# Second block: transposing and normalising rows in one product with a diagonal matrix

## The chip, the cores and the metric

The program runs on 1 core of one Trainium2 chip. The metric is device time in microseconds (us) of one launch. Engines are named as in the profile: PE is TensorE's matmul, PEld its weight load, DVE VectorE, ACT ScalarE, POOL GpSimd, SP SyncE.

## The reference, cut to what matters

Two transformer blocks run one after the other on 256 tokens of width 1024, in float32. The first block (a convolution branch, a gated linear attention branch, a mixture of 64 experts) ends in a layer norm. The second block normalises its rows three times and multiplies each result by large matrices:

```
def _rmsnorm(x, g):
    x32 = x.astype(jnp.float32)
    y = x32 * lax.rsqrt(jnp.mean(x32 * x32, axis=-1, keepdims=True) + EPS)
    return (y * g.astype(jnp.float32)).astype(x.dtype)

xn = _rmsnorm(x, mix_norm[l]);  h = xn @ w_in[l]          # input projections
...
x = x + merged @ w_out[l]
xn = _rmsnorm(x, ffn_norm[l]);  up = xn @ w_up[l]         # feed-forward
x = x + (jax.nn.gelu(g_ffn) * up[..., D_FF:]) @ w_down[l]
g_ple = jax.nn.sigmoid(_rmsnorm(x, ple_norm[l]) @ w_ple_gate[l])
x = x + g_ple * (p[l] @ w_ple_proj[l])
```

Every row (token) has one factor, 1/sqrt(mean of squares + 1e-6); every column (channel) has one gain. PE contracts over the partition dimension, so the rows, which lie with tokens on partitions, have to be transposed to channels on partitions before each of these products.

## The kernel before

The 256 tokens are two tiles (t = 0, 1) of 128 partitions; `tok(10)` holds the rows x of both, 1024 floats each. The engines run five separate instruction streams in the order in which the code is written and meet by semaphores; there is no scheduler. PSUM is 8 banks of 128 x 512 floats, given to tasks in rotation (`take_bank`, `full`, `wait_full`, `read`).

The second block's normalisation happens in three stages: stage 0 before the input projections (tasks `x2t0` to `x2t3`), stage 1 before the feed-forward (`x3t0` to `x3t3`), stage 2 before the last gate (`x4t0` to `x4t3`). Tasks 0 and 1 are the two halves of 4 channel blocks of tile 0, tasks 2 and 3 those of tile 1. For every stage and tile:

- ACT squares both halves of the rows with a running sum (`rms_square`, L1359) and takes the root (`rms_root`, L1365); DVE scales the first half's sum (`rms_shifted`, L2015) and inverts the root (`rms_inverse`, L2020). The result is one factor per partition.
- The rows are multiplied by that factor, 128 x 512 at a time: on ACT (`rms_scale`, L1371), and for tile 1 of stage 0 on DVE (L2076). Each pass increments the semaphore `xn_half`.
- PE transposes 8 blocks of 128 x 128 (`turn_normed`, L731), 4 to a bank, against the identity; each half waits for its own `xn_half`.
- ACT copies each bank out with the column gain, rounded to the form that PE reads fast (`take_turned`, L1380), and DVE writes what the rounding left (`low_turned`, L2065). That releases the bank, and the next product of PE (`kiwi_k` in stage 0, `fg0_0` in stage 1, `pg0_0` in stage 2, lines L644 and L689) waits for tasks 0 and 2 before its first channel block and for 1 and 3 before its fifth (`as_turned`).

Around them: in stage 0 DVE first finishes the layer norm of the first block (`last_norm`: L2027, L2034, L2038, L2041, L2046), whose tile 1 is interleaved with the factor of tile 0. In stage 1 PE runs the four products `mo0_0`, `mo1_0`, `mo0_1`, `mo1_1` of the output projection, and tile 0 is turned between `mo0_1` and `mo1_1`. In stage 2 tile 0 is turned after `dn1_1`, then PE does 8 matmul instructions of `pp` (L1153), then tile 1, then `pp` again, then `pg`. A product called through `mm` on plain float32 operands appears in the trace as two MATMUL and two LDWEIGHTS instructions; a call of `nc.tensor.transpose` on float32 appears as one of each (the transposes of L731 are 48 calls in the code and 48 records; the products of L1096 are 16 calls and 32 records).

Of the kernel before, what the change touches and what calls it, by code (L numbers as in the profile page):

```python
# [7 lines left out]
ALU = mybir.AluOpType  # L8
# [7 lines left out]
P = 128  # L16
# [131 lines left out]
def build(nc, a, out):  # L148
    with ExitStack() as ctx:
        def sb(name, shape, dt=F32):  # L150
            return ctx.enter_context(nc.sbuf_tensor(name, shape, dt))
# [36 lines left out]
        e_idx = sb("e_idx", [P, TT, 8], U32)  # L188
        over = sb("over", [P, 1], I32)
        bias_dram = nc.dram_tensor("bias_scratch", (NH, 512), F32, kind="Internal").ap()  # L190

# [428 lines left out]
        def _(pe):  # L620
# [102 lines left out]

            def turn_normed(src, pre, stage, t):

                for k in range(2):
                    pe.wait_ge(S("xn_half"), 4 * stage + 2 * t + k + 1)
                    o = take_bank(f"{pre}t{2 * t + k}")
                    for i in range(4):
                        c = 4 * k + i  # L730
                        last = nc.tensor.transpose(o[:, P * i:P * i + P], src[:, t, P * c:P * c + P], ident[:])  # L731
                    full(last, f"{pre}t{2 * t + k}")
# [289 lines left out]
            for t in range(TT):  # L1022
                turn_normed(tok(1), "x2", 0, t)
            kiwi_parts = (kiwi_high.rearrange("p (c n) -> p c n", c=DC),
# [76 lines left out]
            for t in range(TT):  # L1101
# [10 lines left out]
                for k in range(2):  # L1112
                    o = take_bank(f"pv{t}_{k}")
                    for s in range(t + 1):
# [8 lines left out]
            tile_by_tile([unit(1), unit(1)], merged2_parts, "mo", arrive=as_counted("merged_low", 4),  # L1123
                         between={(1, 1): lambda: turn_normed(tok(4), "x3", 1, 0)})
            turn_normed(tok(4), "x3", 1, 1)
            for i in range(6):
# [21 lines left out]
            for t in range(TT):  # L1148
                turn_normed(tok(4), "x4", 2, t)
                for u in range(2):  # L1150
                    o = take_bank(f"pp{u}_{t}")
                    for c in range(2):
                        last = mm(o[:], pT[:, c, P * t:P * t + P], w[:, c, 512 * u:512 * u + 512],  # L1153
                                  start=c == 0, stop=c == 1)
                    full(last, f"pp{u}_{t}")
# [6 lines left out]
        def _(act):  # L1162
# [204 lines left out]

            def rms_scale(stage, t, h):
                cut = slice(512 * h, 512 * h + 512)
                act.wait_ge(S("rms_inverse"), 2 * stage + t + 1)  # L1370
                A(tok(4 if stage else 1)[:, t, cut], tok(10)[:, t, cut], ACT.Copy, scale=rms_factor(stage, t)  # L1371
                  ).then_inc(S("xn_half"), 1)

            def take_turned(pre, js, gain):
# [14 lines left out]
            rms_root(0, 0)  # L1389
            rms_scale(0, 0, 0)  # L1390
            ln_root(1)
            rms_scale(0, 0, 1)
            take_turned("x2", [0], "mix_norm")
# [149 lines left out]
            rms_root(1, 0)  # L1543
            rms_scale(1, 0, 0)
            rms_scale(1, 0, 1)
            wait_read(act, "mo0_1")
# [7 lines left out]
            rms_root(1, 1)  # L1554
            rms_scale(1, 1, 0)
            rms_scale(1, 1, 1)
            take_turned("x3", [2, 3], "ffn_norm")
# [31 lines left out]
            for t in range(TT):  # L1589
                wait_read(act, f"dn1_{t}")  # L1590
                rms_square(2, t, 1)
                rms_root(2, t)
                rms_scale(2, t, 0)
                rms_scale(2, t, 1)
                if t:
                    wait_landed(act, 1, "pg1_1")
                    wait_used(act, "dn1_1")
                    weights_high_half(1, "pg1_1", 0)
                take_turned("x4", [2 * t, 2 * t + 1], "ple_norm")
# [10 lines left out]
        def _(dve):  # L1610
# [406 lines left out]

            def rms_inverse(stage, t):
                dve.wait_ge(S("rms_root"), 2 * stage + t + 1)
                v.reciprocal(rms_factor(stage, t), rms_factor(stage, t)).then_inc(S("rms_inverse"), 1)  # L2020

            def last_norm(t):
# [8 lines left out]
                if t:  # L2031
                    rms_inverse(0, 0)
                dve.wait_ge(S("ln_bn"), 2 * k + 2)
# [36 lines left out]
            low_turned("x2", [0], "mix_norm", 0)  # L2070
            rms_inverse(0, 1)
            dve.wait_ge(S("rms_inverse"), 2)
            dve.wait_ge(S("x2_ready"), 4)
            for h in range(2):
                cut = slice(512 * h, 512 * h + 512)
                ts(tok(1)[:, 1, cut], tok(10)[:, 1, cut], rms_factor(0, 1), None, ALU.mult).then_inc(S("xn_half"), 1)  # L2076
            low_turned("x2", [1, 2, 3], "mix_norm", 0)
# [152 lines left out]
            residual("mo", 1, 0)  # L2230
            rms_inverse(1, 0)
            residual("mo", 0, 1)
            low_turned("x3", [0, 1], "ffn_norm", 1)
            rms_shifted(1, 1)
            residual("mo", 1, 1)
            rms_inverse(1, 1)
            low_turned("x3", [2, 3], "ffn_norm", 1)
# [59 lines left out]
            residual("dn", 1, 0)  # L2297
            rms_inverse(2, 0)
            residual("dn", 1, 1)
            low_turned("x4", [0, 1], "ple_norm", 2)  # L2300
            rms_inverse(2, 1)
            take_pp(0)
# [114 lines left out]
```

## Time and profile before

| | us |
|---|---|
| median of 3 runs | 1723.84 (1721.44 to 1726.67) |
| the profiled execution, its own time | 1723.52 |
| its span | 1721.8 |
| PE busy | 1363.8 (79% of the span) |
| DVE busy, ACT busy, POOL busy | 445.4, 446.4, 608.5 |
| mean granted clock of PE | 0.889 of full speed |
| second block, from the end of the experts to the end | about 1206 to 1721.8 |
| PE's share of the chain that ended last | 65% |

The page lists engines' busy times, groups of instructions with what ended the idle time before them, and the chain of work that ended last. A stage is read in the timeline, which gives start, duration and, in brackets, the idle time of the engine before the row and who ended it.

### The profile page before, as it was taken

What the parts mean: (1) busy time and instruction counts of PE and PEld (TensorE: products, weight loads), DVE (VectorE), ACT (ScalarE), POOL (GpSimd) and SP (SyncE); (2) the same over time, 40 slices, a digit from 0 to 9 for tenths busy, and PEclk for the clock granted to TensorE, in tenths of its full rate; (3) what the DMA queues carried; (4) which work ended last, traced back from release to release, by engine and by line L of the source; (5) the groups of instructions that cost most, each with busy time, mean ns of one, the idle gap of its engine ahead of it and who ended that gap; (6) DMA issues with size and microseconds to landing.
All of it is one profiled execution on the core that took longest, in us unless ns stands there. A gap on an engine that the chain in (4) does not pass through costs nothing.

```text
span 1721.8 us, 21025 instructions
## 1 busy us (share of the span) xinstructions
PE 1363.8 (79%) x8812; PEld 965.2 (56%) x8812; DVE 445.4 (26%) x973; ACT 446.4 (26%) x602; POOL 608.5 (35%) x484
## 2 busy tenths in 40 slices
PE   7999998966647755774667576657799999899998
PEld 7899996433313322331333133212699989788886
DVE  3995545100000000000000000000416643355303
ACT  4454741000000000000000000000548554655534
POOL 6886691000000000000000000000587968698894
PEclk9999998988778878886888788778799999999999
DMA  9443469999999999999999999999445444455551
GB/s 362 155 175 120 174 253 367 405 426 424 427 428 429 429 428 429 428 428 429 429 427 430 429 428 429 427 428 418 163 173 205 157 172 147 147 196 189 182 192 50
DMA packets 46505, 539.52 MB, mean 313 GB/s; under 512 B 4504, under 2 KB 8608, under 8 KB 15200
## 3 DMA queue, kind: packets, MB, share of 16 engines
q1 hardware_dynamic: 43296, 533.00, 75.9%
q0 software_dynamic: 1040, 3.38, 0.5%
q10 hardware_dynamic: 2096, 2.11, 0.4%
q8 instruction: 53, 0.87, 0.2%
q14 instruction: 20, 0.16, 0.0%
HBM read 537.41 MB, written 1.06 MB: 313 GB/s over the span
## 4 chain that ended last, share of the span: by engine, by line
PE 65%; DMA 28%; DVE 2%; ACT 2%; SPq 1%; issue 1%; POOL 1%; DVEq 0%; ACTq 0%
PE bank L644 30%; DMA ring<-in_w 16%; PE bank L897 13%; DMA slab<-in_w 10%; PE bank L877 6%; PE bank L689 5%; PE bank L694 3%; PE bank L957 3%; DMA ring<-in_units 1%; SPq L422 1%; PE bank L946 1%; POOL ring_parts L583 1%; PE bank L916 1%; ACT ring_parts L1187 0%; PE bank L1069 0%
## 5 line engine op out<-in xcount | busy, mean ns | idle before, releaser
L583 POOL TENSOR_TENSOR ring_parts<-ring,ring_parts 128x512 fp32r<-128x512 f32 x448 | 594.5, 1371 | 136.4 <-ACT ring_parts L1187 136.3
L897 PE MATMUL bank<-ring,slab 128*32 128x512 f32 x1472 | 252.5, 669 | 152.5 <-DMA ring<-in_w 79.2
L644 PE MATMUL bank<-slab_parts,ring_parts 128*128 128x256 f32 x2560 | 357.1, 284 | 0.4 <-DVE slab L2185 0.4
L644 PEld LDWEIGHTS bank<-slab_parts,ring_parts 128*128 128x128 f32 x2560 | 336.0, 192 | 2.4 <-DVE slab L2185 1.2
L596 POOL TENSOR_TENSOR slab_parts<-slab,slab_parts 128x1088 fp32r<-128x1088 f32 x1 | 2.5, 2476 | 818.7 <-ACT slab_parts L1319 818.7
L946 PE MATMUL bank<-ring,slab 128*32 128x512 f32 x736 | 139.6, 726 | 142.0 <-DMA ring<-in_w 80.3
L897 PEld LDWEIGHTS bank<-ring,slab 128*32 128x32 f32 x1472 | 68.9, 122 | 316.5 <-issue 315.1
L1187 ACT ACTIVATE ring_parts<-ring 128x2048 fp32r<-128x2048 f32 x114 | 211.9, 1910 | 94.6 <-PE bank L644 92.7
L946 PEld LDWEIGHTS bank<-ring,slab 128*32 128x32 f32 x736 | 37.1, 130 | 228.1 <-issue 227.4
L644 PE MATMUL bank<-ring_parts,slab_parts 128*128 128x512 f32 (+1 forms) x672 | 160.4, 388 | 3.9 <-POOL ring_parts L583 2.9
L1964 DVE TENSOR_TENSOR slab<-slab,bank 128x512 f32<-128x512 f32 x16 | 11.0, 688 | 551.8 <-PE bank L897 551.8
L644 PEld LDWEIGHTS bank<-ring_parts,slab_parts 128*128 128x128 f32 x672 | 125.7, 190 | 31.6 <-POOL ring_parts L583 3.7
L897 PE MATMUL bank<-slab 128*32 128x512 f32 x512 | 128.7, 661 | 1.4 <-DMA ring<-in_w 1.4
L877 PEld LDWEIGHTS bank<-slab 128*128 128x128 f32 x512 | 124.3, 334 | 8.2 <-issue 5.0
L877 PE MATMUL bank<-slab 128*128 128x128 f32 x512 | 123.2, 399 | 1.5 <-DVE slab L1947 1.5
L689 PE MATMUL bank<-slab_parts,ring_parts 128*128 128x512 f32 x384 | 97.9, 397 | 2.1 <-DVE slab_parts L2065 2.1
L644 PE MATMUL bank<-rows_parts,ring_parts 128*128 128x256 f32 x368 | 91.4, 285 | 0.0
L1642 DVE SCALAR_TENSOR_TENSOR bank<-slab,cols,bank 128x255 f32<-128x255 f32 (+28 forms) x232 | 88.0, 464 | 0.1
L1307 ACT ACTIVATE slab<-bank 128x512 f32<-128x512 f32 x16 | 9.6, 597 | 286.1 <-PE bank L897 271.8
L1315 ACT ACTIVATE slab<-bank 128x512 f32<-128x512 f32 x16 | 9.6, 597 | 283.7 <-PE bank L946 283.7
L1972 DVE COPY slab<-bank 128x512 f32<-128x512 f32 x16 | 11.1, 691 | 278.0 <-PE bank L946 278.0
L1303 ACT ACTIVATE slab<-bank 128x512 f32<-128x512 f32 x16 | 9.6, 597 | 271.5 <-PE bank L897 248.8
(312 smaller groups left out, 1322.7 us busy)
## 6 DMA issues: line engine op xcount, KB each, us to landing
ring<-in_w SPq DMA_DIRECT2D x142, 2048.0 KB, 19.8
ring<-in_units SPq DMA_DIRECT2D x59, 2048.0 KB, 8.3
slab<-in_w SPq DMA_DIRECT2D x48, 2048.0 KB, 25.1
ring<-in_units SPq DMA_DIRECT2D x2, 1024.0 KB, 9.1
slab<-in_w SPq DMA_DIRECT2D x2, 1024.0 KB, 21.3
slab<-bias_scratch ACTq DMA_DIRECT2D x2, 1024.0 KB, 8.5
slab<-in_xT SPq DMA_DIRECT2D x1, 1024.0 KB, 5.1
rows<-in_ln_g POOLq DMA_DIRECT2D x2, 512.0 KB, 16.6
```

What stands on the lines that cost most here:

```text
L422: sp.dma_start(slot(step, j), src.rearrange("e (p c) n -> p (e c n)", p=P)).then_inc(S(f"expert_landed{step % 2}{j}"), 16)
L583: ins = g.tensor_tensor(r32(w_q), w_q, r32(high_q), ALU.subtract)
L644: return mm(out_, l, r, start=start and first, stop=stop and last)
L689: mm(o[:].rearrange("p (a t) -> p a t", a=2), r32(high[:, c, cut]), r32(xn3_both[:, :, T * c:T * c + T]), start=c == 0, stop=c == DC - 1)
L694: last = mm(o[:, 0:T], r32(low[:, c, cut]), r32(xn3_parts[0][:, c, :]), start=False, stop=c == DC - 1, skip_group_check=True)
L877: last = mm(b[:, P * (c % 4):P * (c % 4) + P], tok(0)[:, t, c::DC], sel[:, t, :, :].rearrange("p j s -> p (j s)"), start=t == 0, stop=t == 1)
L897: last = mm(b[CAP * j:CAP * j + CAP, :], xg[:, c, CAP * j:CAP * j + CAP], wt[j][c], start=c == 0, stop=c == DC - 1, tile_position=(0, CAP ...
L916: last = mm(gate_bank[CAP * j:CAP * j + CAP, :], xg[:, c, CAP * j:CAP * j + CAP], wt[:, j, i, :], start=c == 0, stop=c == DC - 1, tile_pos ...
L946: last = mm(b[CAP * j:CAP * j + CAP, :], hid_t[:, m, CAP * j:CAP * j + CAP], wt[j][:, 512 * hf:512 * hf + 512], start=m == 0, stop=m == 3, ...
L957: last = mm(acc[t][hf][:], spread[:, P * t:P * t + P], y_sb[:, 512 * hf:512 * hf + 512], start=False, stop=ends, skip_group_check=again)
L1187: A(r32(high), w, ACT.Copy).then_inc(S("high_ready"), 1)
L1642: ins = stt(out_, src[:, c, 0:T - lag], wc, sum_[:, lag:T], ALU.mult, ALU.add)
```

## The change

The passes that scale the rows are gone. Instead DVE multiplies the 128 x 128 identity by the row factors into a new tile, `turner[:, t, :]`, right after it has inverted the root, and PE multiplies the unscaled rows by that diagonal matrix: the result of `rows.T @ diag(factor)` is the transposed and scaled block. The call is `mm`, an ordinary float32 product, in place of `nc.tensor.transpose`. PE waits for `turner_ready` once per tile and no longer once per half.

```
-            def turn_normed(src, pre, stage, t):
-
+            def turn_normed(pre, stage, t):
+
+                pe.wait_ge(S("turner_ready"), 2 * stage + t + 1)
                 for k in range(2):
-                    pe.wait_ge(S("xn_half"), 4 * stage + 2 * t + k + 1)
                     o = take_bank(f"{pre}t{2 * t + k}")
                     for i in range(4):
                         c = 4 * k + i
-                        last = nc.tensor.transpose(o[:, P * i:P * i + P], src[:, t, P * c:P * c + P], ident[:])
+                        last = mm(o[:, P * i:P * i + P], tok(10)[:, t, P * c:P * c + P], turner[:, t, :],
+                                  start=True, stop=True)
                     full(last, f"{pre}t{2 * t + k}")
...
-            def rms_scale(stage, t, h):
-                cut = slice(512 * h, 512 * h + 512)
-                act.wait_ge(S("rms_inverse"), 2 * stage + t + 1)
-                A(tok(4 if stage else 1)[:, t, cut], tok(10)[:, t, cut], ACT.Copy, scale=rms_factor(stage, t)
-                  ).then_inc(S("xn_half"), 1)
-
...
             rms_root(0, 0)
-            rms_scale(0, 0, 0)
             ln_root(1)
-            rms_scale(0, 0, 1)
             take_turned("x2", [0], "mix_norm")
...
             rms_root(1, 0)
-            rms_scale(1, 0, 0)
-            rms_scale(1, 0, 1)
...
             rms_root(1, 1)
-            rms_scale(1, 1, 0)
-            rms_scale(1, 1, 1)
...
                 rms_root(2, t)
-                rms_scale(2, t, 0)
-                rms_scale(2, t, 1)
...
-            def rms_inverse(stage, t):
+            def rms_turner(stage, t):
                 dve.wait_ge(S("rms_root"), 2 * stage + t + 1)
                 v.reciprocal(rms_factor(stage, t), rms_factor(stage, t)).then_inc(S("rms_inverse"), 1)
+                dve.wait_ge(S("rms_inverse"), 2 * stage + t + 1)
+                ts(turner[:, t, :], ident[:], rms_factor(stage, t), None, ALU.mult).then_inc(S("turner_ready"), 1)
...
                 if t:
-                    rms_inverse(0, 0)
+                    rms_turner(0, 0)
                 dve.wait_ge(S("ln_bn"), 2 * k + 2)
...
             low_turned("x2", [0], "mix_norm", 0)
-            rms_inverse(0, 1)
-            dve.wait_ge(S("rms_inverse"), 2)
-            dve.wait_ge(S("x2_ready"), 4)
-            for h in range(2):
-                cut = slice(512 * h, 512 * h + 512)
-                ts(tok(1)[:, 1, cut], tok(10)[:, 1, cut], rms_factor(0, 1), None, ALU.mult).then_inc(S("xn_half"), 1)
+            rms_turner(0, 1)
```

All six calls of `rms_inverse` become `rms_turner`, at the same places.

On DVE in stage 0 (the end of the first block's layer norm for tile 1, interleaved with tile 0's factor) there stands before, `bank` and `rows` being the layer norm's operands and `small` the factors:

```order
L2030 BN_STATS small<-bank 128x6
L2020 RECIPROCAL small<-small 128x1 [waits rms_root]
L2034 BN_AGGR small<-small 128x2 [waits ln_bn]
L2038 SCALAR_TENSOR_TENSOR bank<-bank,small,rows 128x512 [waits ln_stats]
L2015 TENSOR_SCALAR small<-small 128x1 [waits rms_sum]
L2065 SCALAR_TENSOR_TENSOR rows_parts<-bank,cols,slab_parts 128x128 [waits xn_high,bank_full6]
L2020 RECIPROCAL small<-small 128x1 [waits rms_root]
L2076 TENSOR_SCALAR slab<-slab,small 128x512 [waits x2_ready,rms_inverse]
L2076 TENSOR_SCALAR slab<-slab,small 128x512
```

The same places on DVE after the change:

```order
L2020 BN_STATS small<-bank 128x6
L2008 RECIPROCAL small<-small 128x1 [waits rms_root]
L2010 TENSOR_SCALAR turner<-ident,small 128x128 [waits rms_inverse]
L2024 BN_AGGR small<-small 128x2 [waits ln_bn]
L2028 SCALAR_TENSOR_TENSOR bank<-bank,small,rows 128x512 [waits ln_stats]
L2003 TENSOR_SCALAR small<-small 128x1 [waits rms_sum]
L2055 SCALAR_TENSOR_TENSOR rows_parts<-bank,cols,slab_parts 128x128 [waits xn_high,bank_full6]
L2008 RECIPROCAL small<-small 128x1 [waits rms_root]
L2010 TENSOR_SCALAR turner<-ident,small 128x128 [waits rms_inverse]
```

For tile 0 a 128 x 128 instruction has moved in ahead of the layer norm's aggregate for tile 1; for tile 1 it takes the place of two 128 x 512 passes.

On PE in stage 1, with the end of `mo0_1`, the turning of tile 0 and the start of `mo1_1`, there stands before:

```order
L644 MATMUL bank<-ring_parts,slab_parts 128x512 [waits low_ready]
L731 MATMUL bank<-ident,slab 128x128 [waits bank_read1,xn_half]
L731 MATMUL bank<-ident,slab 128x128 x3
L731 MATMUL bank<-ident,slab 128x128 [waits bank_read6,xn_half]
L731 MATMUL bank<-ident,slab 128x128 x3
L644 MATMUL bank<-ring_parts,slab_parts 128x512 [waits high_ready,bank_read7]
```

The same place on PE after the change (each row here is a call; the float32 product is two instructions on the chip):

```order
L645 MATMUL bank<-ring_parts,slab_parts 128x512 [waits low_ready]
L732 MATMUL bank<-turner,slab 128x128 [waits bank_read1,turner_ready]
L732 MATMUL bank<-turner,slab 128x128 x3
L732 MATMUL bank<-turner,slab 128x128 [waits bank_read6]
L732 MATMUL bank<-turner,slab 128x128 x3
L645 MATMUL bank<-ring_parts,slab_parts 128x512 [waits high_ready,bank_read7]
```

Nothing moved against its neighbours; the second half of the tile lost its wait for a pass, and the operand is the diagonal.

## Rows read from the trace of the kernel before

**Rows 1.** The page, engines' busy time: us, share of the span, instructions.
```profile
PE 1363.8 (79%) x8812; PEld 965.2 (56%) x8812; DVE 445.4 (26%) x973; ACT 446.4 (26%) x602; POOL 608.5 (35%) x484
```

**Rows 2.** Groups by line and form, 1190 to 1721 us: busy, mean ns, idle before.
```profile
L731 PE MATMUL bank<-ident,slab 128*128 128x128 f32 x48 | 8.5, 329 | 9.6 <-ACT slab L1371 6.8 <-DVE slab L2076 2.8
L731 PEld LDWEIGHTS bank<-ident,slab 128*128 128x128 f32 x48 | 6.6, 167 | 13.8 <-ACT slab L1371 10.2 <-DVE slab L2076 3.2
L1371 ACT ACTIVATE slab<-slab,small 128x512 f32<-128x512 f32 x10 | 6.8, 716 | 1.4 <-DVE small L2020 1.4
L2076 DVE TENSOR_SCALAR slab<-slab,small 128x512 f32<-128x512 f32 x2 | 0.9, 482 | 0.0
```

**Rows 3.** Chain that ended last, in order of time, stage 0: start, us, what.
```profile
1214.64 0.73 ACT slab L1371
1215.41 1.13 PE bank L731 x4
1216.56 1.14 ACT slab_parts L1380 x4
...
1219.66 0.49 DVE slab L2076
1220.20 1.13 PE bank L731 x4
...
1223.97 31.16 PE bank L644 x240
```

**Rows 4.** Timeline, stage 0: start, us, engine, line; in brackets idle before.
```profile
1215.41 1.97 PE L731 MATMUL bank<-ident,slab 128*128 128x128 f32 x8 [3.53 <-ACT slab L1371]
1216.33 1.41 DVE L2046 SCALAR_TENSOR_TENSOR slab<-bank,small,rows 128x512 f32<-128x512 f32 x2
```

**Rows 5.** Other instructions of these kinds: timeline rows, then single lines' durations, min/median/max ns.
```profile
1376.73 5.41 PE L1096 MATMUL bank<-slab 128*128 128x128 f32 x32
...
1393.49 1.03 PE L1108 MATMUL bank<-ident,slab 128*128 128x128 f32 x8
...
L1069 PE MATMUL bank<-slab,ring x32: 379/379/454, 1306.2 to 1313.0; 128*128 128x256 f32 x32
...
L2096 DVE TENSOR_SCALAR slab<-slab x2: 286/316/347, 1306.2 to 1309.3; 128x128 f32<-128x128 f32 x1, 128x256 f32<-128x256 f32 x1
```

**Rows 6.** Chain that ended last, stage 1.
```profile
1471.34 0.87 PE bank L731 x8
...
1479.71 0.73 ACT slab L1371
...
1488.98 1.84 PE bank L689 x8
```

**Rows 7.** Timeline of PE, stage 1.
```profile
1480.48 1.27 PE L731 MATMUL bank<-ident,slab 128*128 128x128 f32 x8 [2.81 <-ACT slab L1371]
1483.80 3.75 PE L689 MATMUL bank<-slab_parts,ring_parts 128*128 128x512 f32 x8 [2.05 <-DVE slab_parts L2065]
```

**Rows 8.** Stretches: span, busy of PE, PEld, DVE, ACT, POOL; granted clock, DMA share, GB/s.
```profile
1228.00:1229.00 1.00, 1.00 (x6) 1.00 (x6) 0.00 (x0) 0.00 (x0) 1.00 (x1) 0.50 0.00 0
1229.00:1230.00 1.00, 1.00 (x11) 0.78 (x10) 0.00 (x0) 0.38 (x1) 1.00 (x2) 0.95 0.00 0
...
1480.00:1482.00 2.00, 1.27 (x8) 0.84 (x8) 0.00 (x0) 1.87 (x6) 1.73 (x2) 0.92 0.93 393
1482.00:1484.00 2.00, 0.20 (x1) 0.23 (x2) 1.58 (x7) 2.00 (x7) 0.00 (x0) 0.50 0.95 410
```

**Rows 9.** Timeline of PE and two pieces of the chain, stage 2.
```profile
1685.42 1.03 PE L731 MATMUL bank<-ident,slab 128*128 128x128 f32 x8
1690.34 1.27 PE L731 MATMUL bank<-ident,slab 128*128 128x128 f32 x8 [0.45 <-ACT slab L1371]
...
1691.61 3.44 PE bank L1153 x8
...
1695.22 22.05 PE bank L644 x96
```

More of the change, by code:

```diff
@@ L189, in build @@
         over = sb("over", [P, 1], I32)
+        turner = sb("turner", [P, TT, P])
         bias_dram = nc.dram_tensor("bias_scratch", (NH, 512), F32, kind="Internal").ap()
@@ L1022, in _ @@
             for t in range(TT):
-                turn_normed(tok(1), "x2", 0, t)
+                turn_normed("x2", 0, t)
             kiwi_parts = (kiwi_high.rearrange("p (c n) -> p c n", c=DC),
@@ L1123, in _ @@
             tile_by_tile([unit(1), unit(1)], merged2_parts, "mo", arrive=as_counted("merged_low", 4),
-                         between={(1, 1): lambda: turn_normed(tok(4), "x3", 1, 0)})
-            turn_normed(tok(4), "x3", 1, 1)
+                         between={(1, 1): lambda: turn_normed("x3", 1, 0)})
+            turn_normed("x3", 1, 1)
             for i in range(6):
@@ L1148, in _ @@
             for t in range(TT):
-                turn_normed(tok(4), "x4", 2, t)
+                turn_normed("x4", 2, t)
                 for u in range(2):
@@ L2230, in _ @@
             residual("mo", 1, 0)
-            rms_inverse(1, 0)
+            rms_turner(1, 0)
             residual("mo", 0, 1)
@@ L2235, in _ @@
             residual("mo", 1, 1)
-            rms_inverse(1, 1)
+            rms_turner(1, 1)
             low_turned("x3", [2, 3], "ffn_norm", 1)
@@ L2297, in _ @@
             residual("dn", 1, 0)
-            rms_inverse(2, 0)
+            rms_turner(2, 0)
             residual("dn", 1, 1)
             low_turned("x4", [0, 1], "ple_norm", 2)
-            rms_inverse(2, 1)
+            rms_turner(2, 1)
             take_pp(0)
```

## The prediction

> **What bounds the kernel now.** I first read the engines' busy times: PE is busy 79% of the span, the others far less [rows 1]. That says that PE matters, not where. So I went to the groups of the second block, to find the lines that the change touches: 48 transposes, 10 passes on ACT and 2 on DVE [rows 2]. The reader should see two things there. The passes are 7.7 us of busy time, but PE's idle time before the transposes is only 9.6 us in all, and part of that is the chain ahead of the pass, which stays. So even if every wait went with the passes, the whole prize is a few us of 1722. Then I followed the chain that ended last through the three stages, because in a stage the question is who is late. In stage 0 it runs ACT pass, transposes, ACT copy, and for tile 1 DVE pass, transposes, ACT copy, until PE takes over at 1223.97 and stays [rows 3]. In stage 1 tile 0 is turned inside a run of PE work (PE was not waiting, the pass was hidden), tile 1 is on the chain with its ACT pass [rows 6]; around it PE idles 2.81 and 2.05 us [rows 7]. In stage 2 PE reaches tile 0 late and waits 0.45 us for tile 1 [rows 9]. Last, the granted clock of these stretches [rows 8].
>
> **The price of a transpose and of a product.** At full clock 8 transposes take 1.03 us; 16 products of the same size in L1096 and 16 of 256 columns take 5.41 [rows 5]. An instruction overlaps with its follower, so the pace, from start to start, is what counts. For the 8 transposes, with about 0.27 for the last one's own length, it is (1.03-0.27)/7 = 0.108 us. Products on plain float32 are two instructions a call. L1069 shows 256-column ones: 32 starts over 6.8 us, 0.21 apart, 0.38 long. In L1096 5.41-0.38 = 5.03 us lie between the first and the last start; 15 steps of 0.21 off leave 1.8 us for 16 steps behind 128-column ones, 0.11 each [rows 5]. I take half of the 256-column pace, 0.107. So an instruction costs the same, and the product needs two: 0.214 a block against 0.108. A tile of 8 goes from 0.86 to 1.71 us, +0.85. At half clock 8 transposes take 1.97 us, of which I count 0.47 for the last one, 0.214 apart [rows 4]; a product there is 0.43, and a bank of 4 is ready +0.86 later.
>
> Perfetto Trace Analysis in the Trainium skill, section Transposes, speaks against this change: a logical transpose should use the transpose mode and not a standard matmul, since it skips the arithmetic. The glossary (Terms) of the skill's TensorE: Matmul & The Clock Gate calls that mode 4 times faster for FP32. By that figure a tile would cost 8 x 0.43 = 3.5 us and not 1.71, and the sum below would be about +12. The trace's two lines give a ratio of 2.
>
> **What goes.** A pass of 128x512 on ACT takes 0.73 until the first transposes can start, 0.04 later [rows 3]. Its successor is a DVE instruction of 128x128. The nearest row is L2096, the same operation and size, 0.286 us [rows 5]. Between reciprocal and pass the trace has 0.04, and I keep that. So the first product can start 0.73-0.29 = 0.43 us earlier than the first transpose did. For tile 1 of stage 0 the DVE pass of 0.49 on the chain [rows 3] becomes 0.29: 0.20 earlier. Bounds for the new instruction: nothing at all to 0.48 (the four times wider L2076 [rows 2]); 0.29 is nearest in form and is taken.
>
> **Stage 0, all at half clock.** Tile 0: start -0.43, first bank +0.86, so ACT's copy (1216.56 [rows 3]) begins +0.43 later. The new DVE instruction also stands ahead of the layer norm of tile 1 and makes it 0.33 later; its last piece, which ended at 1216.33+1.41 = 1217.74 [rows 4], then ends at 1218.07, while ACT is in its copy until 1216.56+0.43+1.14 = 1218.13. Hidden; uncovered it would cost those 0.33. Tile 1: +0.43 inherited, -0.20 for the pass, +0.86 for the first bank: +1.09 until ACT's copy, DVE's rest and the start of `kiwi_k` at 1223.97. The second bank (+1.7) is ready before ACT is done with the first (a bank takes ACT 1.14 [rows 3]) and waits for nobody else. Behind `kiwi_k` PE is the chain for 31 us at a stretch [rows 3], so +1.09 is passed on. But PE runs at half clock until about 1229.1 [rows 8]. If the clock returns at the same moment, only half of the delay is real work lost, +0.55. I take that: +0.55, with +1.09 as the other end.
>
> **Stage 1.** Tile 0 is turned while PE is the chain, so +0.85 in full; the removed ACT passes there were hidden already. Tile 1: start -0.43; first bank 4 more instructions, +0.43; net 0. The second bank is again behind ACT's copy. Total +0.85.
>
> **Stage 2.** Tile 0: PE was late itself, +0.85. ACT's copy starts +0.43 later, so the root and inverse of tile 1 come +0.43 later and the shorter step to the diagonal gives 0.43 back: the diagonal is ready at 1690.34, as before. PE had been free for some 0.6 us (tile 0 from 1685.42 for 8 x 0.108, then eight instructions of L1153 at 3.44/8 = 0.43, is 1689.73, against the start at 1690.34), so it now gets there at 1689.73+0.85 = 1690.58, 0.24 late. Then +0.85 for the tile, and -0.24 because tile 1 took 1.27 us where tile 0 took 1.03: its second half waited for the second pass, and that wait is gone. Together +0.85 at L1153 and at the last product, which starts at 1695.22 [rows 9]. ACT gains 1.3 us here by the passes that go, and nobody waits for it.
>
> **Sum.** 0.55+0.85+0.85 = +2.25 us. On the profiled execution's own 1723.5 (0.3 below the median of 1723.84) that is 1725.8. What a measurement can tell from no change is about 0.3%, 5.2 us, so this is no measurable change.
>
> **Rival 1: the clock comes back sooner or does not fall.** Half clock costs something in both early stages. In stage 0 PE works from 1223.97 to 1229.1 at half speed, 2.6 us lost. In stage 1 the clock fell at about 1481.7 while PE had been idle for 2.81 us and was turning tile 1 (1.27 us), and stayed down through the next 2.05 us of idling [rows 7, 8]; the first eight of L689 then took 3.75 us against 1.84 later [rows 6, 7], 1.9 us lost. The products put twice the work into these gaps, and the idle times shrink to about 2.4 and 1.8. If both losses went: 2.25-2.6-1.9 = -2.25, 1721.3; if one goes, about 1723.5, which is this rival's time. For it: the gap is nearly closed. Against: in stage 0 the clock stayed at half through both batches of transposes and 5 us of `kiwi_k` [rows 3, 8], so a denser second or two may not be enough. It is still within 0.3%.
>
> The skill's TensorE: Matmul & The Clock Gate, section PE-mode transpose, says that transposes do not count as PE being busy for the clock. By that rule the change replaces work that the clock did not see by work that it sees, and stage 1 would hold full clock. The trace agrees so far as the clock fell after a stretch with nothing but transposes in it; it does not separate that from the idle time around them.
>
> **Rival 2, slower: products do not overlap.** The 96 instructions that replace the 48 transposes each run their full 0.27 us (0.47 at half clock), because the weight load of one no longer hides behind the other. Place: the same three stages. Price: stage 0 two banks of 8, each 0.26 more, +4.1; stage 1 16+8 by 0.165, +4.0; stage 2 32 by 0.165, +5.3; with the sum, +15.7, 1739.2. It decides against me from about 0.06 us more per instruction. Against it stand L1096 and L1069, the same kind of call, at 0.11 and 0.21 [rows 5]. For it only that 128-column products with a new stationary block each time are rare in this trace.
>
> **Rival 3: the removed passes free the chain.** If ACT's queue were the bound of a stage, taking 7.2 us off it would pay up to the 9.6 us of PE's waits [rows 2], 1715. Against it: in stage 1 tile 0 and in stage 2 tile 0 nothing waited for the passes, and elsewhere the wait is for one of two passes, 0.73.
>
> **How the numbers follow.** Forecast (+2.25, anything from +1 to +4 by the bounds of single steps): 0.56. Rival 1: 0.30. Rival 2, with milder forms: 0.08. Rival 3: 0.06. The single runs before scatter by 5 us, which is more than any of the likelier cases, so the range is 1720.5 to 1730. Slower by over 0.3%: rival 2 and a run high in the scatter, 0.10. Faster by over 0.3%: rival 3 and the low end, 0.06. Within: 0.84.
>
> **What would show it.** 96 matmuls and 96 weight loads on the line of the product, 0.107 apart at full clock; a DVE instruction of about 0.29 us before them; `kiwi_k` about 1 us later after its layer norm; in stage 1 the products of tile 0 taking 1.7 us with no wait before them; the last product starting 0.85 us later after `dn1_1`; the granted clock around the start of `fg0_0` still at a half, or not (rival 1). It is wrong if the product's pace is not twice the transposes', or if the time changes by more than 5 us.

## The result, and the profile after

| | before | after |
|---|---|---|
| median | 1723.04 us (22 runs) | 1725.29 us (22 runs) |
| ratio | | 1.0017, 95% interval 1.0009 to 1.0024 |
| profiled execution, span | 1721.8 | 1726.1 |

By the ratio the change costs 2.9 us (1.6 to 4.1 by the interval); the medians differ by 2.25. That is a small loss. Its interval is clear of 1, though the loss is inside the 0.3% that I had called no measurable change.

The page's busy times, to hold against [rows 1]:

```profile
PE 1370.5 (79%) x8860; PEld 974.4 (56%) x8860; DVE 447.2 (26%) x977; ACT 439.6 (25%) x592; POOL 608.4 (35%) x484
```

48 more PE instructions, 6.8 us less on ACT. Groups of the second block, the answer to [rows 2] (busy, mean ns of one, idle before):

```profile
L732 PE MATMUL bank<-turner,slab 128*128 128x128 f32 x96 | 15.3, 326 | 7.7 <-DVE turner L2010 7.7
L732 PEld LDWEIGHTS bank<-turner,slab 128*128 128x128 f32 x96 | 14.4, 235 | 10.8 <-DVE turner L2010 10.5
...
L2010 DVE TENSOR_SCALAR turner<-ident,small 128x128 f32<-128x128 f32 x6 | 4.1, 686 | 0.2
```

The last row is the surprise: 686 ns on average for an instruction that I had put at 290. PE's waits hardly shrank, 9.6 to 7.7 us. Timeline of stage 0 (start, us; answers to [rows 3, 4]), with POOL's row beside it:

```profile
1211.07 6.16 POOL L584 TENSOR_TENSOR ring_parts<-ring,ring_parts 128x512 fp32r<-128x512 f32 x5
...
1213.73 1.14 DVE L2010 TENSOR_SCALAR turner<-ident,small 128x128 f32<-128x128 f32 x1
1214.92 3.72 PE L732 MATMUL bank<-turner,slab 128*128 128x128 f32 x16 [2.60 <-DVE turner L2010]
...
1220.12 0.29 DVE L2010 TENSOR_SCALAR turner<-ident,small 128x128 f32<-128x128 f32 x1
1220.46 2.54 PE L732 MATMUL bank<-turner,slab 128*128 128x128 f32 x16 [1.82 <-DVE turner L2010]
```

The same DVE instruction takes 1.14 us while POOL subtracts and 0.29 us when POOL stands still. The chain through stage 1, against [rows 6]:

```profile
1473.47 1.79 PE bank L732 x16
1475.26 5.47 PE bank L645 x24
...
1482.75 1.20 DVE turner L2010
1483.96 0.04 issue
1484.00 1.49 PE bank L732 x8
...
1488.13 3.64 PE bank L690 x8
```

Tile 0 went from 0.87 to 1.79 on the chain; the diagonal of tile 1 took 1.20 there. And stage 2, against [rows 9]:

```profile
1689.17 1.95 PE L732 MATMUL bank<-turner,slab 128*128 128x128 f32 x16
...
1694.38 1.95 PE L732 MATMUL bank<-turner,slab 128*128 128x128 f32 x16
1696.17 3.60 PE L1155 MATMUL bank<-ring,rows 128*128 128x512 f32 x8
```

PE no longer waits for tile 1. Stretches, against [rows 8] (the column behind POOL is the granted clock):

```profile
1221.00:1222.00 1.00, 1.00 (x11) 1.00 (x10) 0.97 (x4) 0.34 (x2) 0.00 (x0) 0.93 0.00 0
1222.00:1225.00 3.00, 1.72 (x8) 1.46 (x8) 1.84 (x7) 2.75 (x9) 0.00 (x0) 0.50 0.00 0
...
1484.00:1487.00 3.00, 3.00 (x16) 2.88 (x16) 0.25 (x1) 1.14 (x4) 0.00 (x0) 0.61 1.00 421
1487.00:1491.00 4.00, 3.05 (x8) 2.27 (x8) 2.00 (x8) 3.78 (x6) 0.77 (x1) 0.50 0.08 33
```

In stage 0 the clock came back at 1218.45, at the end of tile 0's products, and fell again at 1221.86, within tile 1's products and before `kiwi_k`. It was at half again when `fg0_0` started.

Where a difference of this size sits is only seen by cutting the second block at fixed instructions. The labels e1 to e11 are the experiments of the next section; each row is one profiled execution. The cuts, read from each trace: the first root of the layer norm (ACT), the start of `kiwi_k`, the transpose of `wi` that follows the products of `lx`, the first turning of `x3`, the start of `fg0_0`, the first turning of `x4`, the end. In us:

| kernel | root to kiwi_k | kiwi_k to wi | wi to x3 | x3 to fg0_0 | fg0_0 to x4 | x4 to end | root to end |
|---|---|---|---|---|---|---|---|
| before | 12.63 | 31.09 | 216.11 | 12.63 | 201.62 | 36.37 | 510.4 |
| after | 13.85 | 30.80 | 218.23 | 14.82 | 201.03 | 36.90 | 515.6 |
| e8, the changed kernel again | 14.95 | 31.00 | 216.18 | 15.42 | 199.82 | 36.89 | 514.3 |
| e9, changed kernel, longer POOL pieces | 13.44 | 30.71 | 217.94 | 14.23 | 201.39 | 36.91 | 514.6 |
| e1, products with the identity | 14.55 | 29.12 | 215.54 | 14.95 | 201.63 | 37.19 | 513.0 |
| e2, diagonal on ACT | 13.23 | 28.80 | 215.56 | 14.63 | 199.83 | 36.89 | 508.9 |
| e4, before with product fills | 13.21 | 28.81 | 216.34 | 12.63 | 199.49 | 36.37 | 506.9 |
| e5, before with transpose fills | 12.67 | 28.82 | 217.92 | 12.63 | 199.48 | 36.37 | 507.9 |
| e6, diagonal on ACT, product fills | 14.74 | 28.83 | 217.93 | 13.72 | 199.48 | 36.92 | 511.6 |
| e7, e4 with two more fills | 14.97 | 28.82 | 217.96 | 12.63 | 199.49 | 36.32 | 510.2 |
| e10, changed kernel with transpose fills | 17.66 | 28.80 | 218.11 | 14.54 | 199.47 | 36.91 | 515.5 |
| e11, shorter transpose fills | 12.19 | 28.82 | 216.11 | 12.63 | 199.47 | 36.35 | 505.6 |

The column "wi to x3" holds none of the changed code; it is either about 216 or about 218, with and without the change. So 2.1 of the 5.2 us by which the two first profiles differ is not the change's code. The granted clock accounts for it: in this column the profile of before has one stretch at half clock, the first profile of the changed kernel a longer one and a second (one row of before, two of after):

```profile
1351.98:1355.39 3.41, 3.41 (x18) 3.41 (x18) 2.20 (x1) 3.38 (x6) 3.41 (x3) 0.50 0.95 404
```

```profile
1351.57:1358.39 6.82, 6.82 (x34) 6.82 (x34) 5.18 (x3) 6.79 (x8) 6.82 (x5) 0.50 0.55 235
1399.35:1402.77 3.42, 3.30 (x9) 2.22 (x10) 3.22 (x8) 1.61 (x3) 2.11 (x2) 0.50 0.73 307
```

All profiles of the table that are near 218 have about 10 us at half clock there, except e7, which has fills of its own in this column. So a single profile can be 2 us longer by the clock alone, and the rows below are compared stage by stage.

### The profile page after: what moved, and what is told of

Its sections match the earlier page's. It is cut to its first block, busy times and chain, and to the rows that moved or that the text cites. A ratio compares the mean times of both kernels' runs of the same rounds, so it can differ in the third digit from the quotient of the medians.

```text
span 1726.1 us, 21108 instructions
## 1 busy us (share of the span) xinstructions
PE 1370.5 (79%) x8860; PEld 974.4 (56%) x8860; DVE 447.2 (26%) x977; ACT 439.6 (25%) x592; POOL 608.4 (35%) x484
## 4 chain that ended last, share of the span: by engine, by line
PE 66%; DMA 28%; DVE 1%; SPq 1%; ACT 1%; issue 1%; POOL 1%; DVEq 0%; ACTq 0%
PE bank L645 30%; DMA ring<-in_w 16%; PE bank L899 13%; DMA slab<-in_w 10%; PE bank L879 6%; PE bank L690 5%; PE bank L695 3%; PE bank L959 3%; DMA ring<-in_units 2%; SPq L423 1%; PE bank L948 1%; POOL ring_parts L584 1%; PE bank L732 1%; PE bank L918 1%; ACT ring_parts L1189 0%
## 5 line engine op out<-in xcount | busy, mean ns | idle before, releaser
L899 PE MATMUL bank<-slab 128*32 128x512 f32 x512 | 129.6, 665 | 1.3 <-DMA ring<-in_w 1.3
L1317 ACT ACTIVATE slab<-bank 128x512 f32<-128x512 f32 x16 | 9.6, 597 | 284.9 <-PE bank L948 284.9
L1309 ACT ACTIVATE slab<-bank 128x512 f32<-128x512 f32 x16 | 9.6, 597 | 284.6 <-PE bank L899 271.9
L948 PE MATMUL bank<-slab 128*32 128x512 f32 x280 | 75.1, 710 | 5.4 <-DMA slab<-in_w 4.7
```

The costliest lines, as they stand in the source:

```text
L899: last = mm(b[CAP * j:CAP * j + CAP, :], xg[:, c, CAP * j:CAP * j + CAP], wt[j][c], start=c == 0, stop=c == DC - 1, tile_position=(0, CAP ...
L948: last = mm(b[CAP * j:CAP * j + CAP, :], hid_t[:, m, CAP * j:CAP * j + CAP], wt[j][:, 512 * hf:512 * hf + 512], start=m == 0, stop=m == 3, ...
```

## The experiments

**e1, products with the identity.** Only PE's instruction is changed; the passes stay.

```
-                        last = nc.tensor.transpose(o[:, P * i:P * i + P], src[:, t, P * c:P * c + P], ident[:])
+                        last = mm(o[:, P * i:P * i + P], src[:, t, P * c:P * c + P], ident[:],
+                                  start=True, stop=True)
```

> The kernel before with one thing changed: the 48 transposes are plain float32 products with the identity, 96 matmul instructions; the scaling passes stay. Theory 1 (the products' second instruction is the whole price of the change, what the passes give back is small): the stretch from the start of x3's tile 0 to the start of fg0_0 grows by 0.9 + 0.4 us, stage 0 (from the last BATCH_NORM_STATS2 of tile 1 to the start of kiwi_k) by 1.7 us, stage 2 by 1.1 us, against the kernel before; in all +3.5 to +4 us, ratio 1.0020 to 1.0023, more than the full change (1.0017). Theory 2 (the products are free and the DVE instruction that makes the diagonal is the price): stages as before, ratio 1.0000.

Measured: ratio 1.0005, interval 0.9988 to 1.0022, too wide to tell the theories apart. The stages do: stage 0 +1.9, stage 1 +2.3, x4 to end +0.8. PE's timeline of stage 1:

```profile
1467.28 1.95 PE L731 MATMUL bank<-ident,slab 128*128 128x128 f32 x16
1468.98 5.70 PE L644 MATMUL bank<-ring_parts,slab_parts 128*128 128x512 f32 x24
1477.49 3.78 PE L731 MATMUL bank<-ident,slab 128*128 128x128 f32 x16 [2.81 <-ACT slab L1372]
```

16 instructions in the time of 15 steps of 0.11 at full clock, and twice that for tile 1, which ran at half clock. The wait of 2.81 us is the one of [rows 7]. Theory 2, free products, is refuted; stage 1 exceeds the 1.3 expected, and its tile 1 ran at half clock.

**e2, diagonal on ACT.**

```
-                ts(turner[:, t, :], ident[:], rms_factor(stage, t), None, ALU.mult).then_inc(S("turner_ready"), 1)
+            def act_turner(stage, t):
+                act.wait_ge(S("rms_inverse"), 2 * stage + t + 1)
+                A(turner[:, t, :], ident[:], ACT.Copy, scale=rms_factor(stage, t)).then_inc(S("turner_ready"), 1)
```

It is called right behind each `rms_root`.

> The changed kernel with the diagonal made on ACT, right behind its root and DVE's reciprocal, in place of on DVE. In the changed kernel that DVE instruction took 1.14, 0.29, 0.29, 1.19, 0.93 and 0.29 us in the six places. Theory 1 (the DVE instruction is held up by POOL's subtractions that run at that moment, and ACT is not): the ACT instruction takes 0.3 to 0.4 us in all six places; from the reciprocal to the first product 0.5 us everywhere; stage 0 tile 0 is 0.75 and stage 1 tile 1 0.8 us shorter than in the changed kernel, ratio about 1.0008. Theory 2 (the length is due to the identity or to the wait ahead of the instruction, not to the engine): ACT takes about 1.1 us in the same places, ratio 1.0017.

Measured: ratio 0.9999 (0.9982 to 1.0016). The line of the diagonal, min/median/max, and tile 1 of stage 1:

```profile
L1372 ACT ACTIVATE turner<-ident,small x6: 401/402/405, 1214.6 to 1688.0; 128x128 f32<-128x128 f32 x6
...
1478.80 3.48 PE L732 MATMUL bank<-turner,slab 128*128 128x128 f32 x16 [2.49 <-ACT turner L1372]
```

0.40 us in all six places, also where DVE needed 1.19. PE's wait falls from 3.29 to 2.49 us, the 0.8 that was expected; stage 0 is 0.6 us shorter, not 0.75, and stage 1 as a whole only 0.2 (14.63 against 14.82), since tile 1's products ran at half clock from their start. The interval holds theory 1's 1.0008 and ends just below theory 2's 1.0017; the rows settle it for theory 1.

**e3 and e9, POOL's pieces.** `LOW_PIECES = 8` (0.7 us each) and `LOW_PIECES = 2` (2.3 us each) in place of 4, in the changed kernel.

> The changed kernel with POOL's subtractions cut into 8 pieces a half unit in place of 4, so each takes about 0.7 us and not 1.25. Theory 1 (the DVE instruction waits until the POOL instruction that is running ends): the three long ones (1.14, 1.19, 0.93 us) become at most 0.29 + 0.7 = 1.0 and on average about 0.65; no row over 1.0. Theory 2 (the length has another cause): 1.14, 1.19 and 0.93 stay.

> The changed kernel with POOL's subtractions in 2 pieces of a half unit in place of 4, each about 2.5 us. With pieces of 0.7 us (e3) the DVE instruction was not let in between two of them and waited 5.1 and 6.2 us; with 1.25 us it got in at the end of the running one. Theory 1 (DVE gets in at the end of the running POOL instruction when that one is long enough): the diagonal's instruction takes up to 2.8 us where POOL subtracts, ending with a POOL instruction, and 0.29 elsewhere. Theory 2 (whoever issues back to back keeps the port whatever the length): it lasts until POOL's run of pieces ends, 2.5 to 5 us.

e3: the rows of the diagonal and of POOL beside it, and another DVE line of the first block (e3's rows):

```profile
L2010 DVE TENSOR_SCALAR turner<-ident,small x6: 286/344/6206, 1237.4 to 1739.5; 128x128 f32<-128x128 f32 x6
...
1235.55 6.84 POOL L584 TENSOR_TENSOR ring_parts<-ring,ring_parts 128x256 fp32r<-128x256 f32 x10
...
1237.38 5.11 DVE L2010 TENSOR_SCALAR turner<-ident,small 128x128 f32<-128x128 f32 x1
...
L1740 DVE TENSOR_TENSOR slab<-slab 128x1024 f32<-128x1024 f32 x1 | 20.3, 20290 | 0.0
```

The same line in the changed kernel:

```profile
L1740 DVE TENSOR_TENSOR slab<-slab x1: 2003/2003/2003, 107.5 to 107.5; 128x1024 f32<-128x1024 f32 x1
```

In two of the three places both theories missed. DVE's instruction was not let in between the short POOL instructions; in stage 0 it ended at 1242.49, just after POOL's run of ten (1242.39). It took 5.1 us there and 6.2 us in stage 2, and a two-input DVE instruction in the first block went from 2.0 to 20.3 us. In the third place, stage 1, it was let in, in the middle of a run of eight pieces:

```profile
1516.98 5.54 POOL L584 TENSOR_TENSOR ring_parts<-ring,ring_parts 128x256 fp32r<-128x256 f32 x8 [13.02 <-ACT ring_parts L1189]
...
1520.84 0.40 DVE L2010 TENSOR_SCALAR turner<-ident,small 128x128 f32<-128x128 f32 x1
```

It ended at 1521.24, 0.09 us after the sixth piece (1521.15), as theory 1 has it. The one run of the kernel took 1774.39 us, about 50 more than the changed one. In e9 the rule is simple again:

```profile
1480.42 2.34 POOL L584 TENSOR_TENSOR ring_parts<-ring,ring_parts 128x1024 fp32r<-128x1024 f32 x1
...
1481.93 0.92 DVE L2010 TENSOR_SCALAR turner<-ident,small 128x128 f32<-128x128 f32 x1
```

POOL ends at 1482.76, DVE at 1482.85. All three long ones (0.71, 0.92, 0.54 us) end 0.1 us after a POOL instruction (theory 1), as do the three of the changed kernel, and the kernel's one run took 1726.8 us. Where POOL stood still the instruction took 0.29 us in all these runs. So the cause is shown, in three lengths of POOL's pieces: what holds the diagonal is POOL's subtraction. Why the 0.7 us pieces let nothing in at two places and did at the third stays open.

The Trainium skill says this of the chip in SBUF — State Buffer, section Who interferes with whom: `tensor_scalar` may run in a mode that takes the port pair which DVE and GpSimd share, and whoever issues second is blocked until the first is finished. The trace agrees at 1.25 and 2.34 us a piece; at 0.7 us DVE was blocked for longer than the one instruction in two places of three. The mode itself stands in no row.

**e4 and e5, PE's waits filled on the kernel before.** Throwaway products of the identity with ones (e4), or twice as many transposes (e5), into a bank that is written again afterwards (`take_bank` waits until the bank is free; e5 has `for _ in range(2 * n): nc.tensor.transpose(o[:, 0:P], ones[:], ident[:])` in the loop's place):

```
+            def fill(task, n):
+                o = take_bank(task)
+                for _ in range(n):
+                    mm(o[:, 0:P], ident[:], ones[:], start=True, stop=True)
...
             for t in range(TT):
+                fill("kiwi_k", (9, 7)[t])
                 turn_normed(tok(1), "x2", 0, t)
+            fill("kiwi_k", 5)
...
+            fill("x3t2", 11)
             turn_normed(tok(4), "x3", 1, 1)
+            fill("fg0_0", 8)
```

> The kernel before with its transposes and passes; PE's waits in stages 0 and 1 are filled with throwaway float32 products of the identity with ones (9 before x2's tile 0, 7 before its tile 1, 5 before kiwi_k, 11 before x3's tile 1, 8 before fg0_0), into banks that are overwritten afterwards. Theory 1 (the clock follows what PE does, and half clock costs 2.6 us in kiwi_k and 1.9 us at fg0_0): the granted clock is 1.00 when kiwi_k starts and when fg0_0 starts, the first eight of L689 (now some lines lower) take 1.84 us, and the time falls by 3 to 4 us, ratio about 0.998. Theory 2 (the fills only take PE's time or the clock does not respond): ratio 1.000 to 1.0005, the first eight stay at 3.7 us.

> The same fills as e4, in the same places and of the same total length, but made of transposes of ones (two for each product), on the kernel before. Theory 1 (the clock counts a transpose as it counts a product): as e4, clock 1.00 at the start of kiwi_k and of fg0_0, second block (from the layer norm of tile 1 to the end) 505 us in the profile, ratio about 0.998. Theory 2 (the Trainium skill, TensorE: Matmul & The Clock Gate, section PE-mode transpose: transposes do not count as PE being busy): the clock is at 0.50 when kiwi_k and fg0_0 start, second block 508 to 510 us, ratio about 1.000.

Measured: e4 0.9984 (0.9964 to 1.0003), e5 0.9975 (0.9965 to 0.9986). e5's stretches around `kiwi_k` (start 1225.76) and `fg0_0` (start 1485.13), and its first eight instructions of L689:

```profile
1225.00:1229.00 4.00, 3.24 (x27) 3.17 (x28) 1.54 (x6) 4.00 (x5) 1.81 (x2) 1.00 0.00 2
1480.00:1485.00 5.00, 4.41 (x37) 3.74 (x35) 1.41 (x6) 4.60 (x14) 3.08 (x3) 1.00 0.97 354
1485.00:1489.00 4.00, 3.87 (x21) 3.30 (x22) 0.91 (x4) 4.00 (x3) 2.44 (x2) 1.00 0.16 70
...
1485.13 2.09 PE L689 MATMUL bank<-slab_parts,ring_parts 128*128 128x512 f32 x8 [0.31 <-DVE slab_parts L2074]
```

The clock is full, and the eight take 2.09 us in a view in which they took 3.75 before [rows 7]. `kiwi_k` to `wi` falls from 31.09 to 28.82 and `fg0_0` to `x4` from 201.62 to 199.48, 4.4 us together, in e4 and e5 alike. One profile of each proves little, because e2 shows 28.80 and 199.83 without a fill. What carries the claim is that all six filled profiles (e4 to e7, e10, e11) have 28.80 to 28.83 and 199.47 to 199.49, where before, after, e8, e9, e1 and e2 spread over 28.80 to 31.09 and 199.82 to 201.63, and that e5's ratio is clear of 1 (e4's interval is not).

In stage 1 of e5 PE runs nothing but transposes from the end of `mo1_1` to `fg0_0`, and the clock stayed full (second row above). The section PE-mode transpose of TensorE: Matmul & The Clock Gate in the Trainium skill says that transposes do not count as PE being busy in the same way; for these float32 transposes the measurement decides, and they held the clock as products did.

**e6, e7, e8.** e6 is e2 with product fills (9, 5, 5, 9, 6, in the order of e4's five places). e7 is e4 with two more, `fill(f"pv{t}_0", (8, 4)[t])` ahead of PE's wait for the probabilities. e8 is the changed kernel once more.

> e2 (diagonal made on ACT) with fills by products as in e4 (9, 5, 5, 9, 6). If the clock was the larger part of every difference so far, this ends at e4's time plus what the products cost at full clock: stage 1 from tile 0 to fg0_0 12.6 + 0.85 = 13.5 us, stage 2 10.0, second block 505 to 506 us, ratio 0.998 to 0.999. If the diagonal is worth something of its own on the path, it beats e4: below 505.

> e4 with two more fills, 8 and 4 products while PE waits for the copies of the transposed probabilities. If the low clock behind that wait (3.4 us in e4's profile, from 1391.6) comes from it, it is gone and the second block takes 503 to 504 us; ratio 0.0003 to 0.001 below e4's. If the fills reach past the wait they cost up to 0.5 us and the time is e4's.

> The changed kernel once more, beside the others on one chip. Theory 1 (the cost is products plus the held up DVE instruction, the clock varies from run to run): stage 1 from tile 0 to fg0_0 14 to 15 us, DVE's diagonal again about 0.29 us where POOL stands still and 0.9 to 1.3 us where it subtracts, ratio 1.001 to 1.0025; the moments at which the clock falls differ from those of the first profile.

e6: 0.9976 (0.9965 to 0.9987); stage 1 13.72 and x4 to end 36.92. Its ratio is slightly below the expected 0.998 to 0.999, its second block of 511.6 us is not the 505 to 506: the fill ahead of tile 0 came late (below). By the ratio it can't be told from e4 or e5; by stages it is 1.1 and 0.5 us behind them in stages 1 and 2, so the diagonal shows no worth of its own on the path. e7: 0.9981 (0.9970 to 0.9993), not to be told from e4, and its low stretch near 1394 stayed. It is no test of that stretch, because the first of its two new fills did not run in the wait:

```profile
1392.79 2.54 PE L727 MATMUL bank<-ones,ident 128*128 128x128 f32 x16 [1.89 <-DVE slab L2195]
```

PE idled 1.89 us ahead of the fill, and 1.99 us in e4 ahead of the product that it was to precede, for the same DVE line; the fill ran behind the wait and cost time. e8: 1.0011 (0.9998 to 1.0023), a smaller loss than the first 1.0017 and not clear of 1 by itself, and the diagonal's line, against 1.14 and 1.19 us in the first profile:

```profile
L2010 DVE TENSOR_SCALAR turner<-ident,small x6: 285/608/1303, 1211.1 to 1689.8; 128x128 f32<-128x128 f32 x6
```

The hold-up repeats in the same three places (1.30, 1.19 and 0.93 us). The clock does not: here it was at half from before the layer norm until `kiwi_k` was nearly done, and full at `fg0_0`.

**e10, the changed kernel with the clock held, and e11, a shorter fill.** e10 uses pairs of transposes (9, 5, 5, 9, 6); e11 is e5 with 2 in place of 9 ahead of the first tile.

> The changed kernel with PE's waits filled by throwaway transposes (9, 5, 5, 9, 6 pairs), so that the clock is held and its luck drops out. If products and the held up diagonal are the net price: stage 1 from tile 0 to fg0_0 about 14.0 us against 12.6 in e5 (0.9 for tile 0's second instructions, 0.4 to 0.8 for the diagonal), stage 2 10.0 against 9.8; clock 1.00 at kiwi_k and fg0_0; ratio 0.998 to 1.000, 0.001 above e5's 0.9975.

> e5 with 2 pairs in place of 9 ahead of x2's tile 0: in the profiles with fills the loading of their instructions left PE idle for 0.9 to 2.7 us and tile 0 came up to 2.5 us late where the layer norm was early. If that costs: from the layer norm's root to kiwi_k 12.6 us or less also there, ratio at or below e5's 0.9975. If the early fills are needed for the clock: kiwi_k at 0.50, stage 0 2 us longer, ratio 0.9985.

e10: 0.9995 (0.9984 to 1.0006). Tile 1 of stage 1 in e10, then the same in e6, both at full clock:

```profile
1483.30 2.05 PE L737 MATMUL bank<-turner,slab 128*128 128x128 f32 x16 [1.35 <-DVE turner L2019]
1487.12 2.09 PE L690 MATMUL bank<-slab_parts,ring_parts 128*128 128x512 f32 x8 [0.46 <-DVE slab_parts L2064]
```

```profile
1479.18 2.05 PE L737 MATMUL bank<-turner,slab 128*128 128x128 f32 x16 [0.49 <-ACT turner L1381]
1483.00 2.09 PE L690 MATMUL bank<-slab_parts,ring_parts 128*128 128x512 f32 x8 [0.43 <-DVE slab_parts L2071]
```

Stage 1 costs 12.63 with transposes, 13.72 with products and the diagonal on ACT, 14.54 with the diagonal on DVE: 1.1 us for the products, 0.8 for the hold-up. The expectation's 14.0 was low. Its ratio lies in the range given, but 0.0020 above e5's and not 0.001. The 17.66 of e10 and the 14.74 of e6 come from the fill ahead of tile 0: with the layer norm early, its 18 instructions, most of them at half clock, were still running when the diagonal was ready. From their first to tile 0 passed 4.8 us in e10 and 4.5 in e6, of which PE stood idle for 0.76 and 0.33, waiting for nothing that the timeline shows (2.71 in e4). The DMA rows show something there: in each of e4 to e7 and e10 the queue marked "instruction" (q8) moves one packet of 16 KB before the gap ends, and PE goes on 1.2 to 1.5 us after that packet is in. In e4 the packet starts at 1210.34, inside the gap of 1210.06 to 1212.77 (DMA view of 1209 to 1213 us):

```profile
q8 instruction: 1, 0.02, 1.7%
```

That fits PE waiting for its own instructions to be loaded, as e11's expectation has it; no run tests it by itself. e11 shortens the fill:

```profile
1480.54 2.09 PE L689 MATMUL bank<-slab_parts,ring_parts 128*128 128x512 f32 x8 [0.31 <-DVE slab_parts L2074]
...
1222.00:1226.00 4.00, 3.02 (x25) 3.02 (x26) 1.75 (x7) 4.00 (x5) 1.60 (x2) 1.00 0.01 2
```

From the layer norm's root to `kiwi_k` it takes 12.19 us, with the clock full at `kiwi_k`. Its ratio is 0.9973 (0.9960 to 0.9985), median 1716.70 us beside 1721.45 for the kernel before: ahead of both kernels, and not to be told from e5's 0.9975. It keeps transposes and passes.

## Why the prediction was right

The forecast was +2.25 us and no measurable change; measured were +2.9 by the ratio, and 1725.29 lies in the range and 0.5 from the 1725.8. The outcome was right; two of its terms were not, and that the total came so near is in part luck. The two hold-ups on the path, 1.75 us, were missing from the sum. In the first profile about as much was given back by things that were not forecast: a bank of stage 0 at full clock (0.8 us), a shorter stretch behind `fg0_0` (0.6) and stage 2 (0.3). The 0.3% was too coarse as well: with 22 runs each the interval is 2.6 us wide in all, and +2.9 stands clear of no change.

- **The price of a product: right.** Two instructions a block, 1.67 us between the first and the last of 16, which is 0.111 each; 0.107 was forecast. A tile costs +0.92 on the chain where +0.85 stood. Rival 2 (products that don't overlap) is out. So is, for this case, the factor of 4 for FP32 that the Trainium skill gives in TensorE: Matmul & The Clock Gate, section Terms: the measured ratio is 2.
- **The diagonal's instruction: mis-sized, and outside its bounds.** I took 0.29 from one row and bounded it at 0.48. It was 0.29 in three places and 1.14, 1.19 and 0.93 in three, of which the first two are on the path: 0.85 and 0.90 more than the term. A row for this stood in the trace of before and I had passed it over, the same operation on 128x128 and on 128x256 while POOL subtracts:

```profile
L2120 DVE TENSOR_SCALAR slab<-slab x2: 1050/1153/1256, 1319.2 to 1338.2; 128x128 f32<-128x128 f32 x1, 128x256 f32<-128x256 f32 x1
```

- **Stage 0: +1.09 before the clock, measured +1.22 and +2.3 (e8).** In e8 all of it ran at half clock: 1.09 plus 1.01 for the hold-up (1.30 us there for the 0.29) is 2.1, and 0.2 stays unexplained. In the first profile the first bank of the second tile ran at full clock and was ready only 0.05 later, not 0.86. One step was wrong without consequence: I wrote that the second bank is ready before ACT is done with the first. At half clock eight instructions take 8 x 0.214 = 1.71 us and ACT 1.14; in e8 ACT idled 0.57 us for it, and `kiwi_k`'s start does not wait for that bank. Against +1.22, `kiwi_k` to `wi` gave back 0.29 and not the 0.55 credited to the clock.
- **Stage 1: +0.85, measured +2.2.** By the chain: +0.92 tile 0, +0.47 from the end of `mo1_1` to the first product (-0.43 forecast, the hold-up is the difference), +0.81 until the first bank was full (+0.43 forecast, the clock fell meanwhile).
- **Stage 2: +0.85, measured +0.53.** Tile 1 starts 5.21 us after tile 0, before 4.92: +0.29 for the 0.24 forecast. Behind it I wrote that nobody waits for what ACT gains. The last product did: from L1153's start of tile 1 to the second instruction of `pg` it was 4.07 us before and is 3.66.
- **Rival 1, the clock, half right.** That the clock is worth several us is shown by e5 and e11. That denser products bring it back at a given place is not: at `kiwi_k` it was at half in both profiles of the changed kernel and in e9, and full in e1, e2 and e3; at `fg0_0` it was at half in the first profile, e1 and e9, and full in e8, e2 and e3. Over many runs something of it is there: the mean granted clock was 0.890 in the 29 runs of the kernel before beside e2 and 0.893 in e2's own 12, and 0.890 in the 29 beside e8 and 0.892 in e8's 12. From 0.8902 to 0.8923 (e8) is, as an estimate, 2 x 0.0021 x 1722 = 7 us fewer at half clock in a run. So the products did gain some clock, at places that no run pins down; the credit of 0.55 us at `kiwi_k` was 0.29 in one profile and 0.09 in the other. Rival 3 is refuted: 6.8 us less on ACT paid at most 0.4 us.

Adding the stages of the first profile's table gives 0.93+2.19-0.59+0.53 = 3.1 us (and 2.1 us more in the untouched middle), e8's give 3.7; the ratio says 2.9, and e8's 1.9 (-0.3 to 4.0). They agree within what one profile of each can tell. What stays open is where the single run's scatter of 8 us comes from. The clock has a part in it: in the 29 runs of before beside e8 the slower runs tend to be those with the lower mean granted clock (correlation -0.76).

## What to carry to other kernels

A transpose replaced by a float32 product doubled PE's instructions here; such a change pays only where the pass that it saves is itself late, and here the wait for the pass was one of 0.7 us behind a chain that stayed. Before a new DVE instruction with SBUF operands goes on a path, look at what POOL does at that very moment, and take its price from rows of the same operation under the same neighbour; ACT made the same tile in 0.40 us everywhere. Where PE waits before a long run of matmuls, look at the granted clock behind the wait: transposes nobody reads, put into the waits of two stages, gave 4.7 us (e11), more than the change cost. Check in the trace that a fill runs inside the wait: e7's did not.

## What the runs showed of the hardware that was not expected

- DVE was mostly not let in between POOL instructions of 0.7 us: 5.1, 6.2 and, in the first block, 20.3 us for instructions of 0.29 and 2.0 (e3); at one place it got in after 0.40 us. With pieces of 1.25 and 2.34 us it got in at the end of the running one each time (after, e9).
- Float32 transposes held the clock at full (e5, e11), as products did (e4).
- PE stood idle for 0.3 to 2.7 us inside unrolled fills of 18 instructions, after 14 of them, with no wait in the program, and went on 1.2 to 1.5 us after a 16 KB packet of the instruction queue was in (e4 to e7, e10).
